# Output projection by seven products of half sums, weight sums in place

## The chip, the cores and the metric

One core of one Trainium2 chip runs one layer of a hybrid block in 32-bit floats. The metric is device time in microseconds (us) of that core. Engines: PE (TensorE, matrix products; PEld loads its weights), DVE (VectorE), ACT (ScalarE), POOL (GpSimd), SP (SyncE, which here only issues DMAs).

## The reference, cut to what matters

S = 512 tokens, D = 2048, D_FF = 8192.

```python
mixed = (sigmoid(gate_a) * (ya @ w_branch_rnn) + sigmoid(gate_b) * (yb @ w_branch_attn))
h = x + mixed @ w_out                        # 512x2048 by 2048x2048
u = rms_norm(h, norm_mlp_g)
h = h + square(relu(u @ w_mlp_up)) @ w_mlp_down
return rms_norm(h, norm_final_g)
```

## The kernel before, in words

**Split products.** Every factor x is split in two fp32r parts, a rounded one (`hi`, an ACT copy) and the rest (`lo`, a DVE subtraction). A product is three matmuls: hi by hi, hi by lo, lo by hi.

**Stages.** Input projections, recurrence and attention come first. Then gate b with the attention branch: four blocks of six units. A unit is 48 matmuls of 512 columns. `gate_b` adds the result to `mix` (16 chunks of 128 features by 512 tokens, 112 to 144 KB of the partition).

**Output projection** (`project`, `token_unit`, lines 1527 to 1562): 4 blocks of 512 output columns by 4 units of 512 features, 48 matmuls each. Weights land in `raw`, ACT casts them (L634), DVE subtracts (L1035). `mix` is rounded before (L824, L833, L1270, L1288). `out_sums` (L1314) adds the product to h, which POOL's queue loaded from x (L568), and stores it to `h_d` (L571) for the down pass. In the last block's units PE also turns h (`turn_h`, L1578), 8 chunk pairs; ACT copies each scaled by the norm's gain (L842), DVE forms four sums (L1296 to L1303), ACT rounds (L847), DVE subtracts (L1307). ACT squares h for the norm (L854).

**Up pass**: 32 units, each one 256-column strip of `w_mlp_up`, by the Strassen-Winograd scheme: seven products of sums of half blocks instead of eight. A's sums are `shi`/`slo` (made once), B's sums of weights are formed by DVE per unit (L1337) through a spare buffer `up_e`. One product is 24 matmuls of 256 columns. ACT casts part j (L901) as soon as PE has finished the product four before it; four buffers (`uwhi`, `uwlo`) stand in turn. The result of the unit before is put together on the way: ACT snapshots of PSUM banks (L880 to L891), DVE `hid_out` (L1370 to L1375), ACT relu and squares (`hid_act`, L911 to L919), POOL's four half sums (`hid_sums`, L575 to L580), ACT rounding (L923), DVE `hid_lo` (L1379). SP spills these to DRAM (`sums_d`).

The DVE order of one unit i, of which the numbers of the list below are the parts j:

```python
hid_out(i-1, 0); add e=b11+b12; lo 0; add b11=e+b22; lo 1; hid_out(i-1, 2); add b12=b12+b22
lo 2; lo 3; add e=b11+b21; lo 4; lo 5; lo 6; hid_lo(i-1)
```

**Down pass**: 8 groups of 512 hidden features by 2 halves of the output columns, 16 steps. A step is seven products in two halves each (m = 0 to 13, j = m // 2); a half product is 12 matmuls of 512 columns. Seven buffers `dhi`/`dlo`, so ACT and DVE may be seven half products ahead. Sums of A come from `sums_d` (`dsum`). PSUM banks: j is put in A, C, A, B, A, C, A. So a product must wait until what stood in its bank has been read: j = 2 for DVE's `dn_sum` of product 0 (`s.dn_v`), j = 4 and 5 for ACT's two read-outs `dn_out` of products 1 and 2 (`s.dn_a`, L954), j = 6 for the read-out of product 4, which ACT makes at m = 2 of the next step. POOL adds the read-outs to the output (L598). DVE's order in a step: at m = 0 the sum of the last step's product 3, at m = 6 of its product 6, at m = 8 of this step's product 0. In this text, counting from one, the half product m = 4 is the fifth, m = 8 the ninth and m = 12 the thirteenth.

**What sets the order.** Each engine runs its own list, written out by hand, in order; semaphores join them. SP waits in its list before each DMA, so a late condition holds all that is behind. POOL's list: `load_bd`, masks, loads and stores of h, `hid_sums`, then, after the last spill has landed, `dn_adds`.

**Stage changes before.** Projection to up pass: two pairs of chunks are finished while PE stands. Up to down pass: `load22`, `load21` and the sums wait for space, and ACT's first read-out waits for POOL's `sem_inc(s.dn_p, 2)` behind the last spill.

Of the kernel before, what the change touches and what calls it, by code (L numbers as in the profile page):

```python
# [11 lines left out]
P = 128  # L12
S = 512
# [14 lines left out]
RXW = S + PAD  # L28

# [16 lines left out]
U_ML = U_WO + 16  # L46
PAIRS = D_FF // 256
KP = KD // 2
GROUPS = PAIRS // 4

# [7 lines left out]
B_ML = B_WO + 16  # L58
# [37 lines left out]
class Semaphores:  # L96


    def __init__(self, nc):
# [12 lines left out]
        self.h_in = nc.alloc_semaphore("h_in")  # L112
# [43 lines left out]
        self.mix_hi = nc.alloc_semaphore("mix_hi")  # L156
        self.mix_lo = nc.alloc_semaphore("mix_lo")
        self.h_sp = nc.alloc_semaphore("h_sp")
# [6 lines left out]
        self.st_add = nc.alloc_semaphore("st_add")  # L165
# [35 lines left out]
def hybrid_block(nc, x, g_mix, w_in, conv_w, conv_b, w_r, b_r, w_i, b_i, lam, w_br, w_ba, w_out,  # L201
# [13 lines left out]
    mhi = at("mhi", 48, [P, KD, S], F32R)  # L215
    mlo = at("mlo", 80, [P, KD, S], F32R)
# [34 lines left out]
    h = at("h", R4, [P, TT, D], F32)  # L251
    sqjunk = [at("sqjunk0", 140, [P, S], F32), at("sqjunk1", 46, [P, S], F32)]
# [18 lines left out]
    hraw = hs[0]  # L271
    hhi = at("hhi", 197, [P, 7, HALF], F32R)
    hlo = at("hlo", 190, [P, 7, HALF], F32R)
    dhi = [at(f"dhi{k}", ring[k], [P, 2, S], F32R) for k in range(7)]
    dlo = [at(f"dlo{k}", ring[k] + 4, [P, 2, S], F32R) for k in range(7)]
    d11 = [at("d11_0", 0, [P, 4, S], F32), at("d11_1", 184, [P, 4, S], F32)]
    d12 = [at("d12_0", 8, [P, 4, S], F32), at("d12_1", 192, [P, 4, S], F32)]
    d21, d22 = at("d21", 72, [P, 4, S], F32), at("d22", 112, [P, 4, S], F32)
    dn_e = [at("dn_e0", 140, [P, 2, S], F32), at("dn_e1", 136, [P, 2, S], F32)]
    dn_at = [144, 152, 120, 64, 56, 48, 40]  # L280
    dsum = [at(f"dsum{q}", dn_at[q], [P, 2, 4, HALF], F32R) for q in range(7)]
    dshi, dslo = ([v[:, c] for v in dsum] for c in range(2))
# [1578 lines left out]
```

## Time and profile before

| | us |
|---|---|
| median of 3 runs | 2670.2 (2670.16 to 2670.95) |
| the profiled execution | 2670.39, span 2668.6 |
| PE / DVE / ACT / POOL busy | 2599.9 / 1653.1 / 1149.5 / 470.3 |
| mean granted TensorE clock | 0.992 of full |
| DMA | 394.4 MB, 148 GB/s over the span |

The span runs from the first to the last instruction on the core; the time of a run is taken around it. In a timeline each row is one instruction, or several alike: start in us, length in us, engine, line, operation, output<-inputs, count, and in brackets the idle time before it and what ended that. Matmul starts lie 0.227 us apart where the row gives 0.39 as length, since they overlap.

### The profile page before, as it was taken

What the parts mean: (1) busy time and instruction counts of PE and PEld (TensorE: products, weight loads), DVE (VectorE), ACT (ScalarE), POOL (GpSimd) and SP (SyncE); (2) the same over time, 40 slices, a digit from 0 to 9 for tenths busy, and PEclk for the clock granted to TensorE, in tenths of its full rate; (3) what the DMA queues carried; (4) which work ended last, traced back from release to release, by engine and by line L of the source; (5) the groups of instructions that cost most, each with busy time, mean ns of one, the idle gap of its engine ahead of it and who ended that gap; (6) DMA issues with size and microseconds to landing.
All of it is one profiled execution on the core that took longest, in us unless ns stands there. A gap on an engine that the chain in (4) does not pass through costs nothing.

```text
span 2668.6 us, 37358 instructions
## 1 busy us (share of the span) xinstructions
PE 2599.9 (97%) x14116; PEld 2245.1 (84%) x14116; DVE 1653.1 (62%) x1665; ACT 1149.5 (43%) x1429; POOL 470.3 (18%) x320
## 2 busy tenths in 40 slices
PE   7999999999999999999979999999997999999998
PEld 6777878888888888888879999999996788888886
DVE  4436855433333332342377777777777899999996
ACT  4323345412232232232355565556554455555555
POOL 1000010000000000000002223223322343434343
PEclk9999999999999999999999999999998999999999
DMA  4222222222222222234335655665568565445651
GB/s 172 80 94 79 95 98 96 81 95 93 89 84 80 79 95 94 94 111 139 128 111 184 213 195 177 205 207 177 193 213 328 206 229 195 177 186 219 236 205 79
DMA packets 247375, 394.41 MB, mean 148 GB/s; under 512 B 8832, under 2 KB 156880, under 8 KB 238864
## 3 DMA queue, kind: packets, MB, share of 16 engines
q1 hardware_dynamic: 243024, 378.17, 41.2%
q0 software_dynamic: 3344, 9.96, 1.1%
q10 hardware_dynamic: 944, 5.42, 0.5%
q8 instruction: 42, 0.69, 0.1%
q14 instruction: 21, 0.17, 0.0%
HBM read 326.28 MB, written 67.11 MB: 147 GB/s over the span
## 4 chain that ended last, share of the span: by engine, by line
PE 69%; issue 22%; POOL 5%; DMA 2%; DVE 2%; ACT 1%; POOLq 0%; DVEq 0%; ACTq 0%; SPq 0%
PE stream L1529 15%; PE stream L1531 15%; PE stream L1530 15%; PE aux L1827 4%; PE aux L1829 4%; PE aux L1828 4%; POOL hs L575 3%; PE stream L1829 3%; PE stream L1828 3%; PE stream L1827 3%; POOL hs L578 1%; DMA d<-in_w_mlp_down 1%; DMA sums_d<-hlo 1%; PE aux L1709 1%; PE aux L1529 0%
## 5 line engine op out<-in xcount | busy, mean ns | idle before, releaser
L1035 DVE TENSOR_TENSOR wlo<-raw,whi 128x2048 fp32r<-128x2048 f32 (+1 forms) x113 | 258.1, 2284 | 541.4 <-ACT whi L634 541.3
L1529 PE MATMUL stream<-uhi,whi 128*128 128x512 f32 (+1 forms) x1312 | 513.4, 391 | 1.5 <-ACT rx L704 0.8
L1531 PE MATMUL stream<-uhi,wlo 128*128 128x512 f32 (+1 forms) x1312 | 507.6, 387 | 0.0
L1530 PE MATMUL stream<-ulo,whi 128*128 128x512 f32 (+1 forms) x1312 | 507.6, 387 | 0.0
L634 ACT CAST whi<-raw 128x2048 fp32r<-128x2048 f32 (+1 forms) x113 | 215.3, 1906 | 534.3 <-PE stream L1531 533.7
L598 POOL TENSOR_TENSOR hh<-hh,dn_tmp 128x512 f32<-128x512 f32 x124 | 237.0, 1932 | 373.2 <-ACT dn_tmp L954 373.2
L1529 PEld LDWEIGHTS stream<-uhi,whi 128*128 128x128 f32 (+1 forms) x1312 | 245.1, 187 | 58.9 <-issue 7.5
L1531 PEld LDWEIGHTS stream<-uhi,wlo 128*128 128x128 f32 (+1 forms) x1312 | 245.0, 187 | 50.6
L1530 PEld LDWEIGHTS stream<-ulo,whi 128*128 128x128 f32 (+1 forms) x1312 | 245.2, 187 | 49.3 <-issue 1.0
L1791 PE MATMUL stream<-shi,uwhi 128*128 128x256 f32 x896 | 255.5, 285 | 10.1 <-DVE slo L1307 10.1
L1792 PE MATMUL stream<-slo,uwhi 128*128 128x256 f32 x896 | 254.4, 284 | 0.0
L1793 PE MATMUL stream<-shi,uwlo 128*128 128x256 f32 x896 | 254.3, 284 | 0.0
L1791 PE MATMUL aux<-shi,uwhi 128*128 128x256 f32 x896 | 254.3, 284 | 0.0
L1792 PE MATMUL aux<-slo,uwhi 128*128 128x256 f32 x896 | 253.7, 283 | 0.0
L1793 PE MATMUL aux<-shi,uwlo 128*128 128x256 f32 x896 | 253.7, 283 | 0.0
L1472 DVE TENSOR_TENSOR dlo<-d,dhi 128x1024 fp32r<-128x1024 f32 x160 | 232.9, 1472 | 19.9 <-ACT dhi L987 19.9
L987 ACT CAST dhi<-d 128x1024 fp32r<-128x1024 f32 x160 | 167.6, 1053 | 178.2 <-PE aux L1829 109.5
L1827 PE MATMUL stream<-dhi,dsum 128*128 128x512 f32 x448 | 175.7, 392 | 14.0 <-DVE hh L1414 13.6
L1791 PEld LDWEIGHTS stream<-shi,uwhi 128*128 128x128 f32 x896 | 172.8, 193 | 10.8 <-DVE slo L1307 10.3
L1827 PE MATMUL aux<-dhi,dsum 128*128 128x512 f32 x448 | 175.6, 392 | 5.9 <-DVE hh L1414 5.9
L575 POOL TENSOR_TENSOR hs<-h,hs 128x256 f32<-128x256 f32 x32 | 94.2, 2944 | 472.0 <-ACT hs L919 472.0
L1828 PE MATMUL stream<-dlo,dsum 128*128 128x512 f32 x448 | 175.3, 391 | 0.8 <-issue 0.8
(254 smaller groups left out, 5191.9 us busy)
## 6 DMA issues: line engine op xcount, KB each, us to landing
raw<-in_w_in SPq DMA_DIRECT2D x80, 1024.0 KB, 5.0
d<-in_w_mlp_down SPq DMA_DIRECT2D x64, 1024.0 KB, 8.1
dsum<-sums_d SPq DMA_DIRECT2D x56, 1024.0 KB, 8.0
up_a<-in_w_mlp_up SPq DMA_DIRECT2D x32, 1024.0 KB, 6.1
up_b<-in_w_mlp_up SPq DMA_DIRECT2D x32, 1024.0 KB, 8.4
sums_d<-hhi SPq DMA_DIRECT2D x32, 896.0 KB, 5.3
sums_d<-hlo SPq DMA_DIRECT2D x32, 896.0 KB, 7.1
raw<-in_w_out SPq DMA_DIRECT2D x16, 1024.0 KB, 5.1
```

The costliest lines, as they stand in the source:

```text
L598: pool.tensor_tensor(v, v, dn_tmp[r][:], ALU.add).then_inc(s.dn_p, 1)
L634: nc.scalar.copy(whi[slot][:, 0:width], raw[slot][:, 0:width]).then_inc(s.hi_ready, 1)
L1035: V.tensor_tensor(wlo[slot][:, 0:width], raw[slot][:, 0:width], whi[slot][:, 0:width].bitcast(F32), ALU.subtract).then_inc(s.lo_ready, 1)
L1472: V.tensor_tensor(dlo[m % 7][:], parts[j], dhi[m % 7][:].bitcast(F32), ALU.subtract).then_inc(s.dn_lo, 1)
L1529: T.matmul(dst, ah, bh, start=first and k == 0, stop=False)
L1530: T.matmul(dst, ah, bl, start=False, stop=False)
L1531: ins = T.matmul(dst, al, bh, start=False, stop=last and k == n - 1)
L1791: T.matmul(dst, wh, sh, start=opens and q == 0, stop=False, skip_group_check=not opens)
L1792: T.matmul(dst, wh, sl, start=False, stop=False, skip_group_check=not opens)
L1793: ins = T.matmul(dst, wl, sh, start=False, stop=q == KP - 1, skip_group_check=not opens)
L1827: T.matmul(dst, sh, wh, start=opens and i == 0, stop=False, skip_group_check=not opens)
L1828: T.matmul(dst, sh, wl, start=False, stop=False, skip_group_check=not opens)
```

## The change

It computes the output projection as the down pass computes its product, and shares the code.

- `project`, `token_unit`, `out_sums`, the rounding of `mix` to `mhi`/`mlo` and POOL's loads and stores of h go.
- `mix` is turned in half sums, pair by pair (8 pairs of chunks, k = 0 to 7): `mix_raw` (ACT, three copies to `mraw`), `half_sums` (POOL, four), `mix_hi` (ACT, `mshi`), `mix_lo` (DVE, `mslo`, in the place of `mraw`), then two DMAs to `wsums_d`. The buffer is free for the next pair when these have landed. Pairs 0 to 5 are done during gate b, pairs 6 and 7 in the first of four steps of the projection.
- The projection is WG = 2 groups by 2 halves of the columns, `dn_pe`, `dn_act`, `dn_dve`, `dn_adds` with a `Stage` object that names its buffers.
- Sums of weights are made in the place of `b11` and `b12` (no `up_e`, no `dn_e`), each for both halves at once; in a `first` step `dn_sum` of product 0 stands at m = 6 instead of 8.
- `turn_h` in the order TURNS; six of eight pairs' sums by POOL, two by DVE. The first two products of the up pass are begun with six pairs.
- SP stores h in two DMAs of 2 MB in all; the squares for the norm are made in the up pass from 16 loads of 256 KB (`hq_load`, groups 1 to 4).
- Other buffers, hence other orders of the loads at both stage changes.

```diff
         # SP, ahead of the projection
+        for k in range(2):
+            sp.wait_ge(s.ms_sp[k], 16 * 2 * 2)
+        sp.wait_ge(s.quarter, 4 * (U_WO - 2))
+        load_sums(WOUT, wsums_d, 0, 0)
+        load_sums(WOUT, wsums_d, 0, 1)
+        load22(w_load, WOUT, 0, 0)
...
+        sp.wait_ge(s.quarter, 4 * U_WO)
+        sp.dma_start(h[1][:], x_t[:, :, 1024:2048]).then_inc(s.h_in[1], 16)
+        for k in (6, 7):
+            sp.wait_ge(s.ms_lo, k + 1)
+            for c, v in ((0, mshi), (1, mslo)):
+                sp.dma_start(wsums_d[1, :, :, c, k - 4].rearrange("q p n -> p q n"),
+                             v[:].bitcast(F32)).then_inc(s.ms_end[k - 6], 16)
+        for k in range(2):
+            sp.wait_ge(s.ms_sp[k], 32 * 3)
+            sp.wait_ge(s.ms_end[k], 32)
+        load11(w_load, WOUT, 0, 1)
+        load12(w_load, WOUT, 0, 1)
+        step_loads(w_load, WOUT, wsums_d, 0, 0, True)
...
         # SP, start of the down pass (after the sums of the last unit)
+        load_sums(DOWN, sums_d, 0, 2)
+        sp.wait_ge(s.ss2_ok, 2 + 16)
+        load21(d_load, DOWN, 0, 0)
...
+        load_sums(DOWN, sums_d, 0, 6)
+        load11(d_load, DOWN, 0, 1)
         spill(GROUPS - 1, 3)
         for t, half in ((0, 0), (2, 1), (0, 1), (2, 0)):
             load_h(1, t, half)
         for k in range(2):
             sp.wait_ge(s.hs_sp[k], 32 * (PAIRS // 2))
-        load11(0, 1)
-        load12(0, 1)
+        load12(d_load, DOWN, 0, 1)
...
         # POOL
+        pool.sem_inc(s.dn_p, 2)
+        dn_adds(WOUT, 0, 0, begins=True, between=lambda: mix_sums(7))
+        dn_adds(WOUT, 0, 1, begins=True)
+        dn_adds(WOUT, 1, 0)
+        dn_adds(WOUT, 1, 1, flush=True)
...
+        pool.sem_inc(s.dn_p, 4)
...
         # ACT
+        def mix_raw(k):
+            act.wait_ge(s.mix_ok, 2 * k + 2)
+            if k == 0:
+                act.wait_ge(s.yb_lo, KR)
+            else:
+                act.wait_ge(*((s.ms_end[0], 32) if k == 7 else (s.ms_sp[(k - 1) % 2], 32 * ((k - 1) // 2 + 1))))
...
+        def dn_act(S, g, n, free=None, hooks={}):
...
+                if m in hooks:
+                    hooks[m]()
...
+                if m == 10:
+                    dn_out(S, g, n, 1)
+                if m == 12:
+                    dn_out(S, g, n, 2)
...
+        dn_act(WOUT, 0, 0, free=w_free, hooks={3: lambda: mix_raw(6), 5: lambda: mix_hi(6),
+                                               10: lambda: mix_raw(7), 12: lambda: mix_hi(7)})
...
         # ACT, up pass
-                    act.wait_ge(s.up_add, 4 * i + {1: 1, 2: 2, 4: 3, 6: 4}[j])
+                    act.wait_ge(s.up_add, 4 * i + {1: 1, 2: 3, 4: 2, 6: 4}[j])
                 nc.scalar.copy(uwhi[(7 * u + j) % 4][:], parts[j]).then_inc(s.up_hi, 1)
...
+                if j == 5 and square is not None:
+                    square()
...
         # DVE
+                if m == (6 if first else 8):
+                    dve.wait_ge(s.dn_mm, 14 * st + 9)
+                    for sem in early:
+                        dve.wait_ge(sem, 16)
+                    dn_sum(S, g, n, 0, 0)
...
+        dn_dve(WOUT, 0, 0, first=True, early=(s.h_in[0],),
+               hooks={2: lambda: mix_quads(3), 7: lambda: mix_lo(6), 13: lambda: mix_lo(7)})
...
         # DVE, up pass
                 if j == 0:
                     dve.wait_ge(s.up_a[u % 2], loaded)
-                    if not isinstance(n, int) or n:
-                        dve.wait_ge(s.up_lo, n)
-                    add(0, up_e[:], b11, b12)
                 if j == 1:
                     dve.wait_ge(s.up_b[u % 2], loaded)
                     dve.wait_ge(s.up_lo, n + 1)
-                    add(1, b11, up_e[:], b22)
+                    add(0, b11, b11, b12)
+                    add(1, b12, b12, b22)
                 if j == 2:
-                    add(2, b12, b12, b22)
+                    dve.wait_ge(s.up_lo, n + 2)
+                    add(2, b11, b11, b22)
+                    if not first:
+                        hid_out(i - 1, u - 1, 2)
                 if j == 4:
-                    dve.wait_ge(s.up_lo, n + 2)
-                    add(3, up_e[:], b11, b21)
+                    dve.wait_ge(s.up_lo, n + 3)
+                    add(3, b11, b11, b21)
...
         # PE
+        dn_pe(WOUT, 0, 0)
+        dn_pe(WOUT, 0, 1)
+        dn_pe(WOUT, 1, 0)
+        dn_pe(WOUT, 1, 1, flushed=(s.w_end, 4), after={5: 0, 7: 1, 9: 2, 11: 3})
+        for q in range(4, 8):
+            turn_h(q)
```

(`add(k, ...)` waits, for k over 0, for `s.up_add` of the add before it, before the change and after.)

## Rows read from the trace of the kernel before

**Rows 1.** The page, its head and part 1.

```profile
span 2668.6 us, 37358 instructions
...
PE 2599.9 (97%) x14116; PEld 2245.1 (84%) x14116; DVE 1653.1 (62%) x1665; ACT 1149.5 (43%) x1429; POOL 470.3 (18%) x320
```

**Rows 2.** Tile mhi, products: min, median, max ns; first and last start.

```profile
L1529 PE MATMUL stream<-whi,mhi x256: 388/389/477, 1174.0 to 1355.8; 128*128 128x512 f32 x128
```

**Rows 3.** By line, 1174 to 1356.5: count | busy us, mean ns | idle.

```profile
L1529 PE MATMUL stream<-whi,mhi 128*128 128x512 f32 x256 | 99.9, 390 | 2.6 <-DVE wlo L1035 2.6
...
L847 ACT CAST shi<-hs 128x1792 fp32r<-128x1792 f32 x6 | 10.2, 1696 | 14.0 <-DVE hs L1303 14.0
...
L854 ACT ACTIVATE sqjunk<-h 128x512 f32<-128x512 f32 x12 | 7.6, 631 | 0.3
L842 ACT ACTIVATE hs<-aux,par 128x256 f32<-128x256 f32 x18 | 7.2, 467 | 9.9 <-PE aux L1578 9.8
L1578 PE MATMUL aux<-ident,h 128*128 128x128 f32 x48 | 5.7, 272 | 0.0
```

**Rows 4.** Timeline of PE, projection to up pass.

```profile
1358.54 1.97 PE L1578 MATMUL aux<-ident,h 128*128 128x128 f32 x16 [1.87 <-DVE h L1314]
1370.58 0.58 PE L1791 MATMUL stream<-shi,uwhi 128*128 128x256 f32 x1 [10.07 <-DVE slo L1307]
```

**Rows 5.** Timeline of DVE, one unit of the up pass.

```profile
1791.76 2.03 DVE L1379 TENSOR_TENSOR hlo<-hs,hhi 128x1792 fp32r<-128x1792 f32 x1 [3.85 <-ACT hhi L923]
1793.70 0.42 DVE L1370 TENSOR_TENSOR up_out<-stream,snap_P 128x256 f32<-128x256 f32 x1
1794.03 1.22 DVE L1337 TENSOR_TENSOR up_e<-up_a 128x1024 f32<-128x1024 f32 x1
...
1796.58 1.23 DVE L1337 TENSOR_TENSOR up_a<-up_e,up_b 128x1024 f32<-128x1024 f32 x1 [0.20 <-DVE uwlo L1360]
1797.72 1.22 DVE L1360 TENSOR_TENSOR uwlo<-up_e,uwhi 128x1024 fp32r<-128x1024 f32 x1
...
1806.80 1.31 DVE L1360 TENSOR_TENSOR uwlo<-up_e,uwhi 128x1024 fp32r<-128x1024 f32 x1 [0.38 <-ACT uwhi L901]
1811.96 2.03 DVE L1379 TENSOR_TENSOR hlo<-hs,hhi 128x1792 fp32r<-128x1792 f32 x1 [3.85 <-ACT hhi L923]
```

**Rows 6.** Timeline of ACT, the same unit.

```profile
1797.84 1.05 ACT L901 CAST uwhi<-up_a 128x1024 fp32r<-128x1024 f32 x1 [1.51 <-DVE up_a L1337]
...
1800.78 1.05 ACT L901 CAST uwhi<-up_a 128x1024 fp32r<-128x1024 f32 x1 [0.40 <-DVE up_a L1337]
1801.73 0.84 ACT L911 ACTIVATE up_out<-up_out 128x768 f32<-128x768 f32 x1
...
1805.45 0.37 ACT L891 COPY snap_U<-aux 128x256 f32<-128x256 f32 x1 [0.62 <-PE aux L1793]
```

**Rows 7.** Timeline of POOL, the same unit.

```profile
1803.69 3.33 POOL L575 TENSOR_TENSOR hs<-h,hs 128x256 f32<-128x256 f32 x1 [13.69 <-ACT hs L919]
...
1809.48 0.73 POOL L580 TENSOR_TENSOR hs<-hs 128x256 f32<-128x256 f32 x1
```

**Rows 8.** The page, part 6: DMA issues, KB each, median us to landing.

```profile
up_a<-in_w_mlp_up SPq DMA_DIRECT2D x32, 1024.0 KB, 6.1
...
sums_d<-hlo SPq DMA_DIRECT2D x32, 896.0 KB, 7.1
```

**Rows 9.** Timeline of PE, first two steps of the down pass.

```profile
2044.78 0.77 PE L1827 MATMUL stream<-dhi,dsum 128*128 128x512 f32 x1 [13.60 <-DVE hh L1414]
...
2050.03 0.40 PE L1827 MATMUL stream<-dhi,dsum 128*128 128x512 f32 x1
...
2092.14 0.76 PE L1827 MATMUL aux<-dhi,dsum 128*128 128x512 f32 x1 [5.86 <-DVE hh L1414]
```

**Rows 10.** Timeline of ACT, first step of the down pass.

```profile
2054.34 0.69 ACT L954 ACTIVATE dn_tmp<-stream,small 128x512 f32<-128x512 f32 x1 [13.65 <-POOLq L586]
```

**Rows 11.** Stretches of the down pass start: busy, clock, DMA, GB/s.

```profile
2030.00:2040.00 10.00, 1.18 (x6) 0.64 (x4) 8.64 (x8) 6.13 (x7) 0.00 (x0) 0.82 1.04 404
```

More of the change, by code:

```diff
@@ L330, in hybrid_block @@
     yb_hi, yb_lo = chunks(ybhi), chunks(yblo)
-    m_hi, m_lo = chunks(mhi), chunks(mlo)
     def four(t):
@@ L417, in spill @@
                              v[:].bitcast(F32)).then_inc(s.hs_sp[u % 2], 16)
-        for u in range(4):
+        up_load(0, 0, True)
+        h_store(0)
+        h_store(1)
+        for u in range(1, 4):
             up_load(u, u, True)
-            if u == 3:
-                spill(0, 0)
-        with sp.Fori(1, GROUPS) as g:
+        spill(0, 0)
+        with sp.Fori(1, 5) as g:
             for u in range(4):
@@ new lines, in mix_sums, with mix_spill @@
+        def mix_sums(k):
+            pool.wait_ge(s.ms_raw, 3 * k + 3)
+            half_sums(mraw, mix[:, 2 * k, HALF:S], s.ms_add, 4 * k)
+        def mix_spill(k):
+            pool.wait_ge(s.ms_lo, k + 1)
+            for c, v in ((0, mshi), (1, mslo)):
+                pool.dma_start(wsums_d[k // 4, :, :, c, k % 4].rearrange("q p n -> p q n"),
+                               v[:].bitcast(F32)).then_inc(s.ms_sp[k % 2], 16)
+        for k in range(6):
+            mix_sums(k)
+            mix_spill(k)
+            if k == 3:
+                pool.wait_ge(s.ms_add, 16)
+                pool.dma_start(h[0][:], x_t[:, :, 0:1024]).then_inc(s.h_in[0], 16)
@@ new lines, in _, with dn_adds @@
+        mix_sums(6)
+        def dn_adds(S, g, n, first=False, flush=False, begins=False, between=None):
+            st = 2 * (S.g0 + g) + n
+            for k, (t, j) in enumerate(((2, 1), (0, 2), (2, 4), (0, 5))):
+                if flush and k >= 2:
+                    continue
+                if between and k == 1:
+                    between()
+                for r in range(2):
+                    pool.wait_ge(s.dn_a, 8 + 8 * st + 2 * k + r + 1)
+                    if first and k < 2 and r == 0:
+                        pool.wait_ge(s.h_re[n, t, 1], 16)
+                    if begins:
+                        pool.wait_ge(s.h_in[n], 16)
+                    v = S.out(t + r, n, 1)
+                    pool.tensor_tensor(v, v, S.tmp[r][:], ALU.add).then_inc(s.dn_p, 1)
@@ L875, in up_act @@
             a_old = up_bank(u + 1, 0)[:, 0:HALF]
-            for j in range(7):
+            for j in js:
                 act.wait_ge(s.up_mm, n + j + 1)
+                if first and j < 2:
+                    act.wait_ge(s.dn_mm, 7 + 14 * 3 + [10, 8][j])
+                if first and j == 2:
+                    act.wait_ge(s.h_sp[1], 16)
                 if j == 1 and not first:
@@ L939, in _ @@
+        up_act(0, 0, True, range(2))
+        sum_raw(3)
+        sum_hi(2)
+        sum_hi(3)
+        sum_raw(4)
+        act.wait_ge(s.dn_p, 2 + 8 * 3 + 4)
+        act.sem_inc(s.dn_a, 4)
+        sum_raw(5)
+        sum_hi(4)
+        sum_hi(5)
+        sum_raw(6)
+        sum_raw(7)
+        sum_hi(6)
+        sum_hi(7)
+        up_act(0, 0, True, range(2, 7))
         for u in range(1, 4):
             up_act(0, u, False)
-        with act.Fori(1, GROUPS) as g:
+        with act.Fori(1, 5) as g:
+            for u in range(4):
+                up_act(g, u, False, square=lambda: square(u, g - 1))
@@ L1329, in up_dve @@
+        dn_dve(WOUT, 0, 1, early=(s.h_in[1],))
+        dn_dve(WOUT, 1, 0)
+        dn_dve(WOUT, 1, 1)
+        def up_dve(g, u, first, js=range(7)):
             i = 4 * g + u
```

902 lines of the change are left out of this document (456 added, 446 removed).

## The prediction

> **What bounds the kernel now.** I read the page first, then the output projection by tile and by line, then the timelines of DVE, ACT and POOL in one unit of the up pass, and last the two stage changes on PE.
>
> PE is busy 97% of 2668.6 us [rows 1]; the profiled execution took 2670.4, the runs' median 2670.2, so a sum against the first holds for the second. The output projection is 768 products of 512 columns from 1174.0 to about 1356.2, with 48 transposes (5.7 us) and 2.6 us of waiting [rows 2, 3]: (182.2 - 5.7 - 2.6) / 768 = 0.2265 us each, PE at its pace. Then PE stands 1.87 and, after 16 transposes, 10.07 us until the half sums of the normalised h are rounded [rows 4].
>
> In the up pass PE never waits, a unit taking 7 x 24 products in 20.2 us. But look at the three helpers in one unit [rows 5 to 7]: they form a ring. DVE's `hlo` at 1791.76 opens it, its adds feed ACT's casts, ACT's squares start POOL at 1803.69, POOL's four sums end at 1810.2, and the next `hlo` follows at 1811.96, 20.20 us on. ACT waits 0.62 us for PE in it, at `snap_U` [rows 6]: all the slack that shows. The down pass opens with stops of 13.60 and 5.86 us, both ended by a DVE sum of a first product [rows 9].
>
> **The sum, part by part.** Times are taken from the rows; T is the end of the attention branch (1174.0).
>
> Products: 7/8 of 768 is 672, 96 fewer: **-21.7**.
>
> First step of the new projection. Before, `mix` was rounded while PE went on, and only the last four chunks' rounding stood near its path. Now pairs 6 and 7 of `mix` go one after the other through one buffer (`mraw`, `mshi`), with a write to DRAM between them, and the buffer's place is also that of the next step's weights. I follow the written order; PE takes 2.72 us for a half product (12 matmuls), so an unhindered step ends at T+39.1, PE starting at T+1.0 behind the last `mix` sum.
> - To T+5.1: DVE's adds, ACT's cast of the third half product, then the copies of pair 6 (three of 0.47, overlapped [rows 3]).
> - T+11.6: POOL's four sums, 6.5 beside a working DVE (1803.69 to 1810.2 [rows 7]).
> - T+16.9: rounding 1.7 [rows 3], a cast 1.0, `lo` 1.2, then the sum of the first product, 1.4. PE's fifth half product waits for that sum: its own time was 1 + 4 x 2.72 = 11.9, so it stands 5.
> - T+22.2: two adds, a `lo`, and `mslo`; T+29.3: the write has landed, 7.1 [rows 8].
> - T+41: copies of pair 7 1.2, read-out of a product 1.3, two POOL adds 2.6, sums 4 (four of 0.73 [rows 7] and the waits between; DVE is idle then), rounding 1.7, read-out 1.3, which the ninth half product needs.
> - T+61.6: cast, `lo`, `mslo` 4.1, write 7.1, load of `w11` 6.1 [rows 8], two casts and a read-out 3.3, which the thirteenth needs.
> - T+69.5: two half products and a cold start. That is 2.5: 12 products took 2044.78 to 2050.03 instead of 2.72 us [rows 9], the granted clock at its lower level (1.2 GHz) after PE had stood 13.60.
>
> So the step costs **+30.4** over its 38.1. Bounds: POOL unhindered and DMAs 2 us faster each, +21; POOL blocked throughout and `w11` in a full queue, +37.
>
> The other three steps are 38.1 each. Four groups of 8 transposes, 0.95 each, stand in the last [rows 3].
>
> Last product to the up pass: eight chunks, each copied (1.5), summed (3.8), rounded (1.7) and subtracted (2.0), two or three buffers in turn. Counted from PE's end: chunk 3 ready at 6.4, chunk 5 at 15, the last at 23.5, and add, cast and `lo` of the third product 3.3: 26.8; the first two products (5.8) fit inside, so 21.0 is lost. From T: 69.5 + 114.3 + 3.8 + 21.0 = 208.6. Before: 1370.58 - 1174.0 = 196.6 plus its cold start, half of 2.5: 197.9. Projection and change together: **+10.7**. Bounds -3 and +22.
>
> Up pass, sums in place. `up_e<-up_a` at 1794.03 goes, so the first `lo` starts there, 2.27 after `hlo`. Then add, add, `lo`, add, where the next cast needs the third add; each of the three adds now waits for the instruction just ahead on DVE. Such a wait exists today: the add of 1796.58 has 0.20 idle before it, 1.42 a step instead of 1.14 [rows 5]. So the third add starts at 2.27 + 1.42 + 1.42 + 1.14 + 1.42 = 7.7, the cast 1.26 later as now (1796.58 to 1797.84), at 8.9 where it is 6.1. From there to `relu` 3.5 (3.89 less a wait of 0.40 that goes [rows 6]), to the last cast 3.4 (3.72 to `snap_U` less its 0.62, and 0.27), to its `lo` 1.1: 16.9 instead of 15.04 (1806.80 - 1791.76). If POOL ends behind that `lo` as today, the next `hlo` comes 5.16 later: 22.0. But POOL starts at 14.4 and DVE leaves a gap of 0.8 ahead of its sixth `lo`, so one of the four sums (0.73) should slip in: 21.3, nearest to what the rows show of a gap. **1.1 for each of 31 rings, +34.** Bounds: waits free and two sums in the gap, 20.2 (nothing: PE sets the pace); all blocked, 22.0 (+56).
>
> The rows show a POOL sum of 3.33 us where DVE leaves no gap and one of 0.73 where it does [rows 7]. The Trainium skill (SBUF — State Buffer, "Who interferes with whom") says that a VectorE instruction with two SBUF inputs and a GpSimd one that reads SBUF exclude each other, each for the whole instruction. By that rule, with which the 3.33 agrees, no sum slips in between back-to-back subtractions, and this part is +56 rather than +34. A rule of the Trainium skill speaks the other way: VectorE: DVE Perf Modes, "The DRAIN you can't avoid", has a semaphore between two VectorE operations cost nothing extra. By that rule, with which the 0.20 of [rows 5] doesn't agree, the ring is 0.84 shorter and this part +8.
>
> 16 squares of 0.63 + 0.18 move from ACT's idle time in the projection [rows 3] into 16 units, ahead of the last cast. Hidden if POOL can use the gap, 0.75 each if not: I take 0.3 each, **+5** (0 to 12).
>
> Down pass start. The first product's sum moves ahead of two adds and of the wait for `d21`, so the fifth half product starts some 8 us before 2044.78. But the gain is given back four half products on: POOL still waits for the last spill, and `d11` (1 MB, 2.6 us at 404 GB/s [rows 11]) now stands ahead of it on SP's queue, so it lands near 2057 instead of 2054.3 [rows 10]. ACT's wait of 13.65 goes, but POOL's two adds (2.6) now precede its second read-out: ninth half product near 2060.3, today 2044.78 + 2.5 + 4 x 2.72 = 2058.2, and now after a stop, so with a cold start. The next step's `d22` is asked for before `load11` instead of after two loads and two more half products; the stop of 5.86 and its cold start go. 2.1 + 2.5 - 5.86 - 2.5: **-4** (-10 to +3).
>
> At nothing: the rounding of `mix` during the gates, which takes the place of 32 operations there now and lies beside PE's work; if that cover went, a sigmoid would be late for the next block's first bank, which has 8 us (three quarters of a unit) in hand. The down pass's adds, the same in number, later in a step, under seven buffers of lead. SP's two stores of h and 16 loads of 256 KB behind the spills: if late, they hold the next `up_load`, needed two units on. POOL's two loads and four stores of h go.
>
> Sum: 2670.4 + 10.7 + 34 + 5 - 4 = **2716**.
>
> **Rivals.** (1) **The ring does not bind**: the three waits cost DVE nothing and POOL gets through in the gap. For: DVE does the same adds, and 0.62 of slack shows. Against: the cast comes 2.8 us later and the slack is 0.6. 2670.4 + 10.7 - 4 = 2677, chance 0.24, of which 0.09 within 0.2% (5.3 us, about what a measurement of this kernel can tell from no change) and 0.13 slower. (2) **Faster: the first step's two DRAM round trips are covered**, DMA and POOL being idle there, so the 30 shrink below 10, and the ring is free. It decides if the ninth half product starts before T+30. Against: with every sum at 0.73 I still get 35. 2670.4 + 10.7 - 20.4 - 4 = 2657; 0.11, and 0.01 beside it that the change doesn't do what it says (as many products as before, near 2670). (3) **The ring is blocked throughout**, 22.0 a unit and the squares in full. For: between two subtractions back to back POOL got nothing done today. Against: there is a gap. 2670.4 + 10.7 + 56 + 12 - 4 = 2745; 0.14. My forecast: 0.50, its own range 2700 to 2730.
>
> Range: 2668 (leaves out the second rival and the first's better end) to 2742 (nearly all of the third). Faster 0.13 (0.11 and 0.02 of the first rival's better end), same 0.10, slower 0.77.
>
> **What would show it.** 672 products in the projection; PE idle near 5, 11 and 7 us in its first step, ended by a DVE sum and ACT's read-outs; PE idle about 1 us in each up unit, ended by `uwlo`, `hlo` every 21 us; 26 us to the third up product; no stop before the second down step's fifth half product. I am wrong if up units stay at 20.2, or if the first step ends before T+50.

## The result, and the profile after

The changed kernel takes 2705.57 us (median of 4 runs, 2704.66 to 2706.56) against 2670.18 of the kernel before (2669.16 to 2670.95): ratio 1.0134, 95% interval 1.0121 to 1.0147. It is 35 us slower. The profiled execution has a span of 2704.9 us, 36.3 more than before.

The page's head and part 1 of the changed kernel:

```profile
span 2704.9 us, 37169 instructions
...
PE 2598.3 (96%) x14020; PEld 2235.1 (83%) x14020; DVE 1760.6 (65%) x1717; ACT 1197.7 (44%) x1521; POOL 617.6 (23%) x409
```

PE is busy for as long as before [rows 1], with 96 products fewer. A row counts a product as busy for longer while the clock is low (0.63 us at a granted clock of 0.50, 0.39 at 1.00), so the busy time says nothing here. The stretches below do (busy time and count of products, the clock granted, DMA share, GB/s; 1.00 is the upper level of 2.4 GHz, 0.50 the lower). The first is the projection's first step and the start of its second, the other two are pieces of the first step:

```profile
1174.30:1262.00 87.70, 60.97 (x225) 0.82 0.54 198
1180.00:1190.00 10.00, 10.00 (x38) 0.83 0.95 386
1210.00:1220.00 10.00, 4.38 (x10) 0.50 0.00 0
```

What PE waited for over the whole run (us in total, times, the longest):

```profile
PE aux L1922 <- ACT w_tmp L974: 19.7, 2, 12.7
...
PE aux L1922 <- ACT d_tmp L974: 10.9, 1, 10.9
...
PE aux L1922 <- DVE hh L1449: 7.0, 1, 7.0
PE aux L1944 <- ACT snap_P L1067: 5.8, 14, 0.8
PE stream L1944 <- ACT snap_P L1067: 5.5, 14, 0.4
...
PE stream L1714 <- DVE h L1449: 4.8, 1, 4.8
```

Three kinds are new: ACT's read-outs in the projection (`w_tmp`), ACT's bank copy `snap_P` 28 times in the up pass, whose units had no wait of PE before, and ACT's read-out in the down pass (`d_tmp`), at its ninth half product.

The timeline of PE, where it stood in the projection's first step (first half product, fifth, ninth, thirteenth) and in the second (its fifth):

```profile
1177.25 0.79 PE L1922 MATMUL aux<-w_hi,wsum 128*128 128x512 f32 x1 [2.94 <-DVE ga_tmp L1422]
...
1191.77 0.47 PE L1922 MATMUL aux<-w_hi,wsum 128*128 128x512 f32 x1 [0.47 <-DVE h L1449]
...
1215.62 0.77 PE L1922 MATMUL aux<-w_hi,wsum 128*128 128x512 f32 x1 [12.70 <-ACT w_tmp L974]
...
1236.24 0.77 PE L1922 MATMUL aux<-w_hi,wsum 128*128 128x512 f32 x1 [7.00 <-ACT w_tmp L974]
...
1258.87 0.76 PE L1922 MATMUL stream<-w_hi,wsum 128*128 128x512 f32 x1 [3.61 <-DVE h L1449]
...
1372.35 1.12 PE L1714 MATMUL stream<-ident,h 128*128 128x128 f32 x4 [4.84 <-DVE h L1449]
...
1384.73 0.58 PE L1944 MATMUL aux<-shi,uwhi 128*128 128x256 f32 x1 [5.96 <-DVE slo L1513]
...
1393.30 0.39 PE L1944 MATMUL aux<-shi,uwhi 128*128 128x256 f32 x1 [2.48 <-DVE slo L1513]
...
1396.89 0.36 PE L1944 MATMUL aux<-shi,uwhi 128*128 128x256 f32 x1 [1.90 <-DVE uwlo L1560]
```

T, the end of the attention branch, is 1177.25 - 2.94 = 1174.3. The last four rows are the change to the up pass: transposes that wait for h, the first product, its last two pairs, the third product. They answer to [rows 4].

Where the 36.3 us are, between marks that both traces have (us from the one to the other):

| stretch | before | after | difference | forecast |
|---|---|---|---|---|
| start to T | 1174.0 | 1174.3 | +0.3 | 0 |
| T to the third up product | 204.0 | 222.6 | +18.6 | +10.7 |
| third up product to the down pass's first | 641.0 | 659.9 | +18.9 | +39 |
| from there to the end | 649.6 | 648.1 | -1.5 | -4 |

How far one trace can be read shows in the traces of the experiments below, where a stage that an edit left alone can be held against the same stage here. Of the up pass's +18.9, 1.5 us is in the first unit alone: the clock granted fell to 0.50 once more, from 1398.4 to 1401.8, in the trace of the changed kernel, and was 1.00 there in e4 and e10, which have the same code in this stage. From the second unit to the down pass the difference is 17.4. The down pass's first two steps took 95.7 to 98.7 us in eight traces of the same code there (97.5 in the changed kernel).

### The profile page after: what moved, and what is told of

It reads as the page before. It is cut to its first block, busy times and chain, and to the rows that moved or that the text cites. A ratio compares the mean times of both kernels' runs of the same rounds, so it can differ in the third digit from the quotient of the medians.

```text
span 2704.9 us, 37169 instructions
## 1 busy us (share of the span) xinstructions
PE 2598.3 (96%) x14020; PEld 2235.1 (83%) x14020; DVE 1760.6 (65%) x1717; ACT 1197.7 (44%) x1521; POOL 617.6 (23%) x409
## 4 chain that ended last, share of the span: by engine, by line
PE 67%; issue 23%; POOL 4%; DVE 2%; DMA 2%; ACT 1%; SPq 0%; POOLq 0%; DVEq 0%; ACTq 0%
PE stream L1671 13%; PE stream L1673 13%; PE stream L1672 13%; PE stream L1922 4%; PE stream L1924 4%; PE stream L1923 4%; PE aux L1922 4%; PE aux L1924 4%; PE aux L1923 4%; POOL hraw L651 2%; POOL hraw L648 1%; DMA w<-in_w_out 1%; PE aux L1844 1%; DMA hh<-h_d 0%; PE aux L1671 0%
## 5 line engine op out<-in xcount | busy, mean ns | idle before, releaser
L1190 DVE TENSOR_TENSOR wlo<-raw,whi 128x2048 fp32r<-128x2048 f32 (+1 forms) x97 | 221.4, 2283 | 449.7 <-ACT whi L748 449.7
L687 POOL TENSOR_TENSOR hh<-hh,d_tmp 128x512 f32<-128x512 f32 x124 | 309.0, 2519 | 300.0 <-ACT d_tmp L974 272.3
L748 ACT CAST whi<-raw 128x2048 fp32r<-128x2048 f32 (+1 forms) x97 | 184.8, 1905 | 416.7 <-PE stream L1673 416.0
L1498 DVE TENSOR_TENSOR d_lo<-d,d_hi 128x1024 fp32r<-128x1024 f32 x224 | 306.8, 1405 | 74.5 <-ACT d_hi L1004 74.4
L1004 ACT CAST d_hi<-d 128x1024 fp32r<-128x1024 f32 x224 | 229.4, 1051 | 158.4 <-DVE d L1465 105.9
L1081 ACT CAST uwhi<-up_a 128x1024 fp32r<-128x1024 f32 x160 | 168.7, 1054 | 203.4 <-DVE up_a L1538 201.5
L1560 DVE TENSOR_TENSOR uwlo<-up_a,uwhi 128x1024 fp32r<-128x1024 f32 x160 | 207.7, 1298 | 21.9 <-ACT uwhi L1081 21.9
L1922 PE MATMUL aux<-d_hi,dsum 128*128 128x512 f32 x448 | 176.5, 394 | 17.9 <-ACT d_tmp L974 10.9
L1944 PEld LDWEIGHTS aux<-shi,uwhi 128*128 128x128 f32 x896 | 173.3, 193 | 20.1 <-DVE slo L1513 8.9
L1465 DVE TENSOR_TENSOR d<-d,d 128x1024 f32<-128x1024 f32 x128 | 184.9, 1485 | 4.6 <-DMA d<-in_w_mlp_down 4.6
```

What stands on the lines that cost most here:

```text
L687: pool.tensor_tensor(v, v, S.tmp[r][:], ALU.add).then_inc(s.dn_p, 1)
L1004: nc.scalar.copy(S.hi[m % 7][:], parts[j]).then_inc(s.dn_hi, 1)
L1190: V.tensor_tensor(wlo[slot][:, 0:width], raw[slot][:, 0:width], whi[slot][:, 0:width].bitcast(F32), ALU.subtract).then_inc(s.lo_ready, 1)
L1498: V.tensor_tensor(S.lo[m % 7][:], parts[j], S.hi[m % 7][:].bitcast(F32), ALU.subtract).then_inc(s.dn_lo, 1)
L1922: T.matmul(dst, sh, wh, start=opens and i == 0, stop=False, skip_group_check=not opens)
L1944: T.matmul(dst, wh, sh, start=opens and begin and q == ks[0], stop=False, skip_group_check=not opens)
```

## Experiments

All times are medians. Each was run beside the kernel before on the same chip, whose median was 2670.8 or 2670.9 each time. First the up pass. Here is one unit of it in the changed kernel, DVE:

```profile
1780.44 2.03 DVE L1579 TENSOR_TENSOR hlo<-hraw,hhi 128x1792 fp32r<-128x1792 f32 x1 [2.35 <-ACT hhi L1105]
...
1782.72 1.22 DVE L1560 TENSOR_TENSOR uwlo<-up_a,uwhi 128x1024 fp32r<-128x1024 f32 x1
1784.04 1.23 DVE L1538 TENSOR_TENSOR up_a<-up_a 128x1024 f32<-128x1024 f32 x1
1785.30 1.22 DVE L1538 TENSOR_TENSOR up_a<-up_a,up_b 128x1024 f32<-128x1024 f32 x1
1786.44 1.22 DVE L1560 TENSOR_TENSOR uwlo<-up_a,uwhi 128x1024 fp32r<-128x1024 f32 x1
1787.78 1.23 DVE L1538 TENSOR_TENSOR up_a<-up_a,up_b 128x1024 f32<-128x1024 f32 x1
...
1793.62 1.22 DVE L1560 TENSOR_TENSOR uwlo<-up_a,uwhi 128x1024 fp32r<-128x1024 f32 x1
1795.55 1.66 DVE L1560 TENSOR_TENSOR uwlo<-up_b,uwhi 128x1024 fp32r<-128x1024 f32 x1 [0.72 <-ACT uwhi L1081]
...
1801.25 2.03 DVE L1579 TENSOR_TENSOR hlo<-hraw,hhi 128x1792 fp32r<-128x1792 f32 x1 [2.35 <-ACT hhi L1105]
```

ACT in the same unit:

```profile
1789.04 1.05 ACT L1081 CAST uwhi<-up_a 128x1024 fp32r<-128x1024 f32 x1 [2.69 <-DVE up_a L1538]
...
1791.21 0.37 ACT L1067 COPY snap_P<-stream 128x256 f32<-128x256 f32 x1
...
1793.47 0.84 ACT L1101 ACTIVATE hraw<-up_out 128x768 f32<-128x768 f32 x1
...
1799.53 1.69 ACT L1105 CAST hhi<-hraw 128x1792 fp32r<-128x1792 f32 x1 [2.17 <-POOL hraw L653]
```

POOL, and the stop of PE:

```profile
1794.39 1.04 POOL L648 TENSOR_TENSOR hraw<-h,hraw 128x256 f32<-128x256 f32 x1 [15.70 <-ACT hraw L1101]
1795.40 0.73 POOL L649 TENSOR_TENSOR hraw<-hraw,h 128x256 f32<-128x256 f32 x1
1796.09 1.72 POOL L651 TENSOR_TENSOR hraw<-hraw 128x256 f32<-128x256 f32 x1
1797.89 1.60 POOL L653 TENSOR_TENSOR hraw<-hraw 128x256 f32<-128x256 f32 x1
```

```profile
1791.63 0.38 PE L1944 MATMUL stream<-shi,uwhi 128*128 128x256 f32 x1 [0.39 <-ACT snap_P L1067]
```

`hlo` comes every 20.81 us, 20.20 before [rows 5]. By PE's rows the second to fourth unit still take 20.16 us each; from the fifth on there is a stop in each of the 28 units that are left (two in one of them). The third add, at +7.34, releases the cast at +8.60, which was at +6.08 before. That one makes `snap_P` late, and PE stands. It is reported as 0.39 us. The products on both sides of the stop start 0.67 apart where 0.12 is the pace, so it costs 0.55. PE does not hold up the ring: in these rows PE ends no wait of DVE, ACT or POOL, and they go from `hlo` over the adds, the cast, the squares and POOL's sums to `hhi` and the next `hlo`.

**The squares** (e0). Left out: the squares of h for the norm, whose factor then comes from a constant.

```diff
-                hq_load(u, g - 1)
...
-                up_act(g, u, False, square=lambda: square(u, g - 1))
+                up_act(g, u, False)
```

> The changed kernel without the 16 squares of h in the up pass and without their 16 loads (the norm's factor then comes from a constant). Theory (ring of DVE, ACT and POOL, closed by the in-place adds alone): the period of an up unit stays 20.81 us, in the units that had a square as in those that had none; 2705 us, at most 1 less. Rival (ACT's squares lengthen the ring, as the prediction priced with 0.3 a unit): 16 units get shorter, 2700.

Measured 2705.5 us, the period still 20.81. The squares cost nothing. In the changed kernel's rows above, the cast and the square lie beside POOL's sums, which end later than they do: POOL, not ACT, is what the next rounding waits for (`hhi` at 1799.53, with POOL's last sum ending at 1799.49).

**The spare buffer put back** (e1). The same part left out. The first add stands ahead of the first subtraction again, as before.

```diff
+    up_e = at("up_e", 140, [P, 8, P], F32)
...
-                    add(0, b11, b11, b12)
-                    add(1, b12, b12, b22)
+                    add(0, up_e[:], b11, b12)
+                    add(1, b11, up_e[:], b22)
```

> As the kernel without squares, and the spare buffer of the weight sums put back in the up pass, in the place that the squares' buffers had, with the order of adds of the kernel before (the first unit alone stays in place). Theory (ring): the third part's cast comes at +6.1 instead of +8.6 us after the last subtraction of the unit before, PE no longer waits at the copy of its bank, 20.2 us a unit: 31 x 0.6 = 18.6 less, 2687. Rival (the units are long because spills, loads and the one buffer of half sums collide, whatever the adds' order): stays at 2704 to 2706.

Measured 2686.4 us, 19.1 less than without the squares alone. Timeline of DVE, two units:

```profile
1769.20 2.03 DVE L1593 TENSOR_TENSOR hlo<-hraw,hhi 128x1792 fp32r<-128x1792 f32 x1 [2.35 <-ACT hhi L1106]
...
1789.36 2.03 DVE L1593 TENSOR_TENSOR hlo<-hraw,hhi 128x1792 fp32r<-128x1792 f32 x1 [2.35 <-ACT hhi L1106]
```

20.16 us a unit is 168 products at 0.12: PE sets the pace again.

**In place, alone, in the kernel before** (e2): the reverse edit, and nothing of the other parts of the change.

```diff
-                    add(0, up_e[:], b11, b12)
-                    add(1, b11, up_e[:], b22)
+                    add(0, b11, b11, b12)
+                    add(1, b12, b12, b22)
+                if j == 2:
+                    add(2, b11, b11, b22)
```

> The kernel before with one part of the change alone: the weight sums of the up pass in place, with the changed kernel's order on DVE. Theory (ring): 20.8 us a unit instead of 20.2, 18 to 19 us more than before, 2689. Rival (the half sums' single buffer or the new bank order of the changed kernel is what lengthens a unit): 2670 to 2673.

Measured 2688.4 us, 17.5 more than the kernel before beside it (ratio 1.0066, 1.0049 to 1.0082). Its timeline of DVE and its waits of PE:

```profile
1761.62 2.02 DVE L1380 TENSOR_TENSOR hlo<-hs,hhi 128x1792 fp32r<-128x1792 f32 x1 [2.35 <-ACT hhi L923]
...
1782.43 2.02 DVE L1380 TENSOR_TENSOR hlo<-hs,hhi 128x1792 fp32r<-128x1792 f32 x1 [2.35 <-ACT hhi L923]
```

```profile
PE aux L1792 <- ACT snap_P L885: 5.5, 14, 0.4
```

The same 20.81 and the same wait, without a half sum of the projection or a square in it. From both sides, then: the order of the in-place adds costs 0.6 us a unit from the fifth unit on, and no other part of the change was needed for it.

**A second buffer for the last pair** (e3). Now the projection's first step. Pairs 6 and 7 go through one buffer, and pair 7 waits until pair 6 has landed in DRAM. Here pair 7 gets the places of two half sums of the first group, which SP loads once it has landed. The edit takes two waits away: pair 7 no longer waits for the write of pair 6, and the loads of `w11` and `w12` no longer for the write of pair 7.

```diff
+    mraw7 = at("mraw7", 88, [P, 7, HALF], F32)
+    mshi7 = at("mshi7", 96, [P, 7, HALF], F32R)
...
-            sp.wait_ge(s.ms_end[k], 32)
+        sp.wait_ge(s.ms_end[0], 32)
         load11(w_load, WOUT, 0, 1)
         load12(w_load, WOUT, 0, 1)
+        sp.wait_ge(s.ms_end[1], 32)
+        for q in range(5, 7):
+            load_sums(WOUT, wsums_d, 0, q)
...
         mix_sums(6)
+        mix_sums(7)
...
-        dn_act(WOUT, 0, 0, free=w_free, hooks={3: lambda: mix_raw(6), 5: lambda: mix_hi(6),
-                                               10: lambda: mix_raw(7), 12: lambda: mix_hi(7)})
+        dn_act(WOUT, 0, 0, free=w_free, hooks={3: lambda: (mix_raw(6), mix_raw(7)), 5: lambda: mix_hi(6),
+                                               8: lambda: mix_hi(7)})
...
-               hooks={2: lambda: mix_quads(3), 7: lambda: mix_lo(6), 13: lambda: mix_lo(7)})
+               hooks={2: lambda: mix_quads(3), 7: lambda: mix_lo(6), 8: lambda: mix_lo(7)})
```

> The changed kernel with a second buffer for pair 7 of the half sums of mix, in the place of the sixth and seventh weight-side half sums of the first group (which are loaded once pair 7 has landed). Theory (the first step is one chain through one buffer and two DRAM round trips): pair 7 is formed right behind pair 6, the ninth half product starts near T+34 (41.3 in the changed kernel), the thirteenth at T+45 to T+48 (61.9), the first step ends 16 to 23 us sooner: 2683 to 2690. Rival (the step is bound by its weights and by POOL, whatever buffer there is): the thirteenth half product stays beyond T+58, 2702 or more.

Measured 2689.0 us, 16.6 less than the changed kernel. PE's timeline, fifth, ninth and eleventh half product:

```profile
1192.69 0.47 PE L1930 MATMUL aux<-w_hi,wsum 128*128 128x512 f32 x1 [1.34 <-DVE h L1457]
...
1205.41 0.50 PE L1930 MATMUL aux<-w_hi,wsum 128*128 128x512 f32 x1 [1.60 <-DVE w_lo L1506]
...
1219.64 0.77 PE L1930 MATMUL stream<-w_hi,wsum 128*128 128x512 f32 x1 [8.49 <-DVE w_lo L1506]
```

The ninth half product starts at T+31.1 (41.3 in the changed kernel), but the eleventh stops for 8.5 us. The row names a subtraction of DVE. The load of the sixth half sum speaks against it: SP issued it at 1210.98, behind the write of pair 7, and it took 8.6 us to land, so it was there at 1219.6, when PE went on.

**The read-out first** (e4). On ACT, the read-out of the third product ahead of the rounding of pair 7.

```diff
-                if m in hooks:
+                if m in hooks and not (free and m == 12):
                     hooks[m]()
...
                     dn_out(S, g, n, 2)
+                    if free and m in hooks:
+                        hooks[m]()
```

> The changed kernel with one swap on ACT in the projection's first step: the read-out of the third product ahead of the rounding of pair 7. Theory (one chain through the half sums' buffer sets the thirteenth half product; the ninth only waits beside it): the ninth starts near T+35 instead of T+41.3, the thirteenth stays within 1 us of T+61.9, the stop only moves there, total 2704.5 to 2707. Rival (the stops add up, each is worth its length): 6 us less, 2699.

Measured 2703.9 us, 1.7 less than the changed kernel, and the intervals of the two ratios overlap (1.0107 to 1.0138 here). PE's timeline, ninth and thirteenth half product:

```profile
1209.36 0.76 PE L1924 MATMUL aux<-w_hi,wsum 128*128 128x512 f32 x1 [5.93 <-ACT w_tmp L974]
...
1234.93 0.77 PE L1924 MATMUL aux<-w_hi,wsum 128*128 128x512 f32 x1 [11.69 <-ACT w_tmp L974]
```

T is 1174.7 here: the ninth came at T+34.7, 6.6 us sooner, the thirteenth at T+60.2, 1.7 sooner (within 1 was expected). The first stop shrank from 12.7 to 5.9 and the second grew from 7.0 to 11.7. From T to the third up product this trace is 0.5 us shorter (222.0 for 222.6). A stop that is not the last one on its chain is worth almost nothing.

**The pair's two parts in places of their own** (e8). The rounded part of pair 7 goes out as soon as it is made, and the sixth half sum comes into its place.

```diff
+        sp.wait_ge(s.ms_hi, 8)
+        mix_out(7, 0, mshi7, s.ms_h7)
+        sp.wait_ge(s.ms_lo, 7)
+        mix_out(6, 0, mshi, s.ms_end[0])
...
+        sp.wait_ge(s.ms_h7, 16)
+        load_sums(WOUT, wsums_d, 0, 5)
         load11(w_load, WOUT, 0, 1)
```

> As the kernel with a second buffer for pair 7, but its rounded part alone lies in the place of the sixth half sum and is written to DRAM as soon as it is rounded, so that the sixth half sum is loaded about 7 us sooner (issued near T+30 instead of T+36.6). Theory (the 8.5 us stop before the eleventh half product, at T+45.2 in that kernel, is the wait for this load, not for the DVE subtraction that the row names): the stop shrinks to 0 to 3 us, 2682 to 2685. Rival (it is DVE's subtraction): 2688 to 2690, as without the split.

Measured 2685.4 us, 3.6 less than e3. The stop at the eleventh half product is gone with the earlier load, as the landing time in e3 says: what the row puts down to DVE's subtraction was a load. But at the thirteenth there is one of 2.45, again for a load:

```profile
1219.26 0.77 PE L1937 MATMUL aux<-w_hi,wsum 128*128 128x512 f32 x1 [2.45 <-DMA wsum<-wsums_d]
```

The seventh half sum stands behind the 2 MB of `w11` and `w12`.

**Squares kept, spare buffer too** (e5). The load of h lands in the place of `hhi`, after its spill and before the next rounding. SP's order of loads and spills changes with it.

```diff
+    hq = at("hq", 197, [P, S], F32)
+    up_e = at("up_e", 140, [P, 8, P], F32)
...
+            sp.wait_ge(s.hs_sp[t % 2], 64 * c + 32 * (t // 2 + 1) + 32)
+            sp.dma_start(hq[:], h_d[:, t, bass.ds(512 * c, 512)]).then_inc(s.hq_in[0], 16)
...
+                if j == 6 and square is not None:
+                    square()
                 if j == 6 and not first:
```

> The changed kernel, nothing left out: the squares of h are read into the place of the rounded half sums, between their landing in DRAM and the next rounding, behind the unit's last cast on ACT, so that the spare buffer of the weight sums is there again in the up pass. Theory (ring; a square has room beside POOL's sums): 20.2 us a unit with and without squares, 2687, as the kernel with the spare buffer and no squares (2686.4). Rival (the load of h lands too late, behind two spills of 0.9 MB, and the wait for it enters the ring): the 16 units with squares stay near 20.8 or above, 2696 or more.

Measured 2686.5 us, 20.16 us a unit: what the kernel without squares had, with nothing left out.

**Both** (e9: e5 and e8).

> The split places of pair 7 and the squares in the place of the rounded half sums together, nothing left out of the computation. Theory (the two costs lie in stages one after the other and add up): 2705.6 - 18.6 - 22 = 2665, range 2662 to 2668, below the kernel before (2670.4). Rival (a shorter projection only lengthens the wait at the change to the up pass, or the up pass's load of weights comes late): 2672 or more.

Measured 2668.8 us over 11 runs, ratio to the kernel before 0.9989 (0.9980 to 0.9998). The two gains add up to 39.2 (19.1 and 20.1), and 36.8 came: a little short of the forecast, and faster than the kernel before by 0.02 to 0.2%. Part of the shortfall shows in the trace: from the thirteenth unit on the units of the up pass take 20.2 to 20.3 us, and one takes 21.2, where e5 has 20.16 from the second unit to the last. Why was not tried.

**POOL's adds at once** (e10), in the changed kernel. The wait guards none of their buffers.

```diff
-        pool.wait_ge(s.hs_sp[1], 32 * (PAIRS // 2))
         dn_adds(DOWN, 0, 0, first=True)
```

> The changed kernel without POOL's wait for the landing of the last spill ahead of its adds in the down pass (its buffers have nothing in common with those of the spill). Theory (the ninth half product of the down pass waits for the second read-out, that for POOL's adds, those for the spill, 14.4 us): the stop of 10.95 us goes, the ninth half product starts 10 us sooner, 2695; if the load of d12 behind the spill is next, the second step stops instead and less than 5 us are left of the gain. Rival (the cold start and the loads of the down pass are what costs there, the wait only covers them): 2703 or more.

Measured 2703.0 us, 2.6 less, again with overlapping intervals of the ratios (1.0103 to 1.0136 here). In the changed kernel POOL starts these adds when the spill lands, and the ninth half product follows:

```profile
2094.92 4.95 POOL L687 TENSOR_TENSOR hh<-hh,d_tmp 128x512 f32<-128x512 f32 x4 [27.70 <-DMA sums_d<-hlo]
```

```profile
2074.85 0.77 PE L1922 MATMUL aux<-d_hi,dsum 128*128 128x512 f32 x1 [6.95 <-DVE hh L1449]
...
2098.27 0.76 PE L1922 MATMUL aux<-d_hi,dsum 128*128 128x512 f32 x1 [10.95 <-ACT d_tmp L974]
```

And in e10, DVE ahead of the second step's first subtraction, and PE's stop at that step's fifth half product:

```profile
2101.28 2.36 DVE L1497 TENSOR_TENSOR d_lo<-d,d_hi 128x1024 fp32r<-128x1024 f32 x2 [6.54 <-issue]
```

```profile
2122.51 0.76 PE L1921 MATMUL stream<-d_hi,dsum 128*128 128x512 f32 x1 [8.41 <-DVE hh L1448]
```

The stop of 10.95 us went, and 8.41 came ten half products later. The load of `d12` still stands behind the same spill on SP's queue and was issued at 2093.18. The row of DVE names no releaser, but the first of the loads issued there landed after 8.0 us, at 2101.2, and DVE, whose list waits for `d12` ahead of the step's first subtraction, goes on at 2101.28. PE then waits for the sum that DVE makes after its adds. The first two steps of the down pass took 96.5 us here for 97.5, inside the 95.7 to 98.7 that the same code without this edit took: in the traces the edit is worth 1 us there, which is not clear of their scatter. The median lies at the rival's bound (2703); that the stop of 10.95 went speaks for the theory, and the new stop behind `d12` is the case in which it left less than 5 us.

**All that helped** (e11: e9, e10, the seventh half sum ahead of `w12`, and the sum of the first product at m = 6 in the projection's second step).

> All that helped, together: split places for pair 7 (with the seventh half sum loaded ahead of w12), squares in the place of the rounded half sums with the spare buffer, the sum of the first product at m = 6 in the projection's second step too, and POOL's adds without the wait for the spill. Theory (stops in stages one behind the other add up): 2668.8 less 10 for the wait, less 2 to 5 for the two orders: 2654 to 2658. Rival (the second step of the down pass stops for d12 and the projection's second step for its weights): 2664 or more.

Measured 2665.5 us over 11 runs (2660.8 to 2669.9), ratio 0.9977 (0.9968 to 0.9987): the fastest kernel of the study, clear of the kernel before by 0.1 to 0.3%. It missed its forecast of 2654 to 2658 and fell to the rival (2664 or more), which had the second steps of both passes stop. PE's stops in the down pass:

```profile
2031.16 0.76 PE L1957 MATMUL aux<-d_hi,dsum 128*128 128x512 f32 x1 [6.10 <-DVE hh L1471]
...
2047.51 0.77 PE L1957 MATMUL aux<-d_hi,dsum 128*128 128x512 f32 x1 [2.71 <-ACT d_tmp L993]
...
2081.28 0.76 PE L1957 MATMUL stream<-d_hi,dsum 128*128 128x512 f32 x1 [3.44 <-DVE hh L1471]
```

The 10 us that the forecast took off for POOL's wait did not come: part of the stop moved to the second step, as in e10, and the first two steps took 96.0 us for 96.4 in e9. The way from T to the third up product is 3.8 us shorter than in e9 (200.3 for 204.2), within the 2 to 5 that were expected of the two new orders there. Which of the two brought what was not tried apart.

## Why the prediction was right, and where its sizes were off

It forecast 2716 (2668 to 2742), slower with 0.77. The kernel is slower, and the two costs that it named, the chain through the half sums' buffer and the ring in the up pass, are the two that the experiments show. The total came out 10 us too high because errors of size stood against each other: up pass and squares 20 too high, projection and its change 8 too low, down pass 2.5 too hopeful. That the sum is off by only 10 is partly luck. The two signs that would have shown it wrong stayed away: the units did not stay at 20.2, and the first step ended at T+69.9, not before T+50.

**Products**: 224 rows of each of three kinds in the projection, 672, as forecast.

**The first step**: forecast T+16.9, T+41 and T+61.6 for the fifth, ninth and thirteenth half product, and T+69.5 for its end; measured T+17.5, T+41.3, T+61.9 and T+69.9. The chain in written order, with durations from the rows of before, held within 1 us. The stops themselves were 5, 11 and 7 by forecast, 0.5, 12.7 and 7.0 measured. The first is the one that I had wrong: PE began at T+2.9 and not at T+1.0, and the granted clock was 0.50 from there until 1183.4, so its first 14 products started 0.43 us apart, which is 3.0 more together than at their pace. Both used up what I had priced as a stop. The trace of e1, which has the same code in this stage, shows that the chain and not PE sets the time. There PE began behind a wait of 3.02, its first four half products ran at a granted clock of 1.00, and the fifth started at T+17.6 all the same, behind a longer stop:

```profile
1191.74 0.47 PE L1936 MATMUL aux<-w_hi,wsum 128*128 128x512 f32 x1 [3.37 <-DVE h L1450]
```

That the later stops come from the one buffer is shown by e3: its DRAM writes are no shorter (pair 6 was written from 1198.3 to about 1204.8, in the changed kernel from 1197.4 to about 1203.8), only pair 7 no longer waits for the first of them, nor `w11` and `w12` for the second. Both waits go in one edit and are not priced apart.

**The other steps**: "38.1 each" failed. The first step's late loads left DVE behind in the second, whose fifth half product waited 3.61 us for the sum of its first product. With the slow products behind that stop the second step took 43.4 us, which is most of the 5.6 by which the last product came late (T+193.2 for T+187.6); the third took 38.0. In e3 the second step has no such stop, but in e8 and e9 it has again one of 2.23 and 3.59 us, so I know the place of this stop and not fully what sets it.

**The change to the up pass**: 29.4 us from the last product to the third up product, forecast 26.8. By the rows what is missing in my sum is that PE's own transposes wait for the last sums of h (4.84). Together with the steps before: +18.6 for +10.7, near the upper bound of 22.

**The ring**: the mechanism holds, the size was 0.6 a unit, not 1.1, and 28 units paid it, not 31. PE's stop is not ended by `uwlo`, as I had written, but by ACT's bank copy `snap_P`, which stands behind the late cast in ACT's list. Step by step: third add at +7.34 (7.7 forecast), cast +8.60 (8.9), POOL's start +13.95 (14.4), next `hlo` +20.81 (21.3). Two terms were too large. I charged each of the three waits 0.28 us. The rows give 0.12 between two adds (1.26 apart, 1.14 without a wait) and 0.18 and 0.20 between a subtraction and an add, 0.50 together. And I let one POOL sum slip into DVE's gap. Two did (1.04 and 0.73 us), and POOL's four take 5.1 us where I had 5.8.

The rule of the Trainium skill (SBUF — State Buffer, "Who interferes with whom") that a two-input VectorE instruction and a GpSimd one that reads SBUF exclude each other fits these rows, in both directions: POOL's third and fourth sum take 1.72 and 1.60 instead of 0.73, and the subtraction that met POOL's second sum takes 1.66 instead of 1.22. What I drew from it for the +56 was too hard: a sum that has begun seems to hold DVE in its turn, and so makes room. The rule of the Trainium skill (VectorE: DVE Perf Modes, "The DRAIN you can't avoid") that a semaphore costs nothing extra does not fit: 0.12 to 0.20 us each.

**The squares**: +5 forecast, 0 measured (e0). I had placed them on the ring; they lie beside POOL's part of it.

**Down pass start**: -4 forecast, -1.5 measured. Counted from the pass's first product, the fifth half product starts at +18.0 where it was +25.7 (8 sooner forecast, 7.7 measured), the ninth at +41.4 (forecast 2060.3 - 2019.0 = 41.3), behind the spill as forecast, and the second step's stop is gone. After two steps the pass is 5.6 us ahead of before (97.5 for 103.0). The rest was given back later: 0.7 between the last product and the end, and 3.4 in steps 3 to 16, of which a stop of 0.84 in the last step is one part. The other is at the fifth half product of each step: from the fifth step on a step takes 38.2 to 38.4 us where all took 38.08 before, and PE goes on when DVE's sum of the first product ends, here in the eleventh step:

```profile
2469.41 1.40 DVE L1449 SCALAR_TENSOR_TENSOR hh<-aux,small,hh 128x512 f32<-128x512 f32 x2
```

```profile
2470.87 0.50 PE L1922 MATMUL aux<-d_hi,dsum 128*128 128x512 f32 x1
```

The product before started 0.28 us earlier, not 0.23, so the row shows no wait. All traces with the changed down pass have the 3.4 us (2.4 to 3.6), the two without it have none. "The down pass's adds at nothing" was thus short by some 2.5 us. That their new place in DVE's list does it was not tried.

**The rivals**: that the ring doesn't bind (2677) is ruled out by e1 and e2. That it is blocked throughout (2745) is ruled out by 20.81. The faster rival, round trips covered, had its point of decision at T+30 for the ninth half product: it was T+41.3, and a second buffer was needed to reach T+31.1.

## What to carry to other kernels

When an edit frees a buffer by working in place, look at what the lost buffer let run ahead: here one cast needs three adds instead of two, and a ring of three engines that had 0.6 us of slack pays 0.6 us in each of 28 units. Where data pass one by one through a single buffer with a DRAM write in between, write the chain down in issue order with durations from the trace; it gave the half products within 1 us here, and a second buffer gave back 17 us. A stop is worth its length only if nothing behind it waits for the same thing: two edits took 7 and 11 us of stops away, and their traces show 0.5 and 1 us for it, the medians 1.7 and 2.6, not clear of the changed kernel.

## What the runs showed that I had not expected

- A PE stop reported as 0.39 us costs 0.55: the products around it start 0.67 apart, not 0.12.
- A wait ended by a DMA can be put down to an engine: in e3 the row of an 8.5 us stop names DVE, a load lands just as the stop ends, and e8 takes the stop away by issuing that load sooner.
- A stop and a slow stretch stand in for each other: with the first four half products partly at a granted clock of 0.50 the stop behind them was 0.47 us (changed kernel), with all at 1.00 it was 3.37 (e1), and the product behind it started at T+17.5 and T+17.6. PE had waited 2.94 and 3.02 us before, so the length of that wait does not tell which it will be.
- A DVE subtraction of 1.22 us grows to 1.66 when a POOL sum has begun in the gap ahead of it.
- A landing behind others is far from its median: the last spill of 0.9 MB took 14.4 us to land in the changed kernel, the median of its kind there is 9.1.
